# Last block of a small transformer: TensorE's transposes of five operands against VectorE's 32x32 blocks and transfers

## The chip, the core and the metric

The kernel runs on one core of one Trainium2 chip. The metric is the device time of one execution in microseconds, median of several runs.

## The reference

A sequence of 256 tokens with 1024 features goes through two layers (feed-forward, mixer, feed-forward, gated embedding) and then one hybrid block; everything is float32. The change touches the hybrid block alone:

```python
proj = jnp.einsum("bsd,dc->bsc", h, w_in)            # 1024 -> 10240 columns
xc, bg, cg, zc, q, k, v, za, g_conv, g_attn = jnp.split(proj, splits, axis=-1)
c = causal_depthwise_conv(cg * xc, conv_w)            # width 3, along the sequence
y_conv = jnp.einsum("bsc,cd->bsd", jax.nn.silu(zc) * bg * c, w_out_conv)
o = mixture_of_dilations(q, k, v, slopes)             # 16 heads of 64, three dilations
y_attn = jnp.einsum("bsc,cd->bsd", jax.nn.silu(za) * o, w_out_attn)
g_conv = jax.nn.sigmoid(g_conv + b_merge[:D_MODEL])
g_attn = jax.nn.sigmoid(g_attn + b_merge[D_MODEL:])
merged = g_conv * y_conv + g_attn * y_attn
return jnp.einsum("bsd,de->bse", merged, w_o)
```

At 256 tokens the three dilations reduce to one attention in which each key counts `times` times (a table of 0 to 3).

## The kernel before

**Weights.** All weights stream through one ring of slots; a slot is a 512-column, 512-row piece (1 MB) of some matrix. SP (SyncE's queue) loads a slot into `w_raw` (3 places) in two transfers of 512 KB, as soon as the slot three before it has been split. ScalarE rounds it to float32r (`w_hi`, `round_hi`, 6 places), GpSimd subtracts to get the rest (`w_lo`, `subtract`, four instructions per slot), and TensorE forms every product as three matmuls: high by high, low by high, high by low (`across_tile`: 4 k-tiles x 3 = 12 matmuls of 512 columns for a slot and one of the two token tiles of 128). ScalarE works four slots ahead (`ahead`).

**The hybrid block.** `HI` is the input projection: 20 column groups c of 512, two slots each, so slots 0 to 39 with slot = 2c + j; then `HC`, `HA` and `HO`, four slots each. `H_ORDER` sets which columns come as which c: 0 and 1 are queries, 2 and 3 keys, 4 and 5 values, 6 x 7 and 8 x 9 the convolution's input, 10 x 11 and 12 x 13 the convolution's gate, 14 and 15 the attention's gate, 16 to 19 the merging gates. Slots 0 to 3 are used for tile 0 and then for tile 1; from slot 4 on a slot is used for both tiles in turn, and the same for all engines: each engine's function `hybrid` walks through c and j and does what the tables name there. After a slot from c = 5 on comes `step(k)`, k = 0 to 20: for TensorE the scores of heads k and k + 1 (even k below 16) and the product of head k - 5's weights with the values; for ScalarE the exponentials of head k; for VectorE scores plus distance and maxima of head k, sums and transposition of head k - 1, and the scaling of head k - 5's output. Queues are in order, and semaphores tie them together.

**Transposes.** Eight column groups (`H_UNITS`: c = 0, 1, 2, 3, 7, 9, 11, 13) are needed with features on the partitions. `take(c)` on VectorE moves them from the accumulator to `h_s` (two places, `H_PLACE`). Then, at the places in `H_UNITS_AT`, TensorE's `unit(c, t)` turns four 128x128 blocks into the PSUM bank `tb[:, 1]`, once for each tile. From there ScalarE's `units(c)` copies them (queries, keys, convolution input), or VectorE's `z_units(c)` multiplies them onto the convolution (gate). The next group must wait until the bank is free: `pe.wait_ge(h_pl_ready, w)` or `pe.wait_ge(h_z_ready, w - 12)`.

**Heads.** The attention weights of a head are turned in another way already. VectorE turns 32x32 blocks of 128x384 into `h_pb`, which holds a pair of heads (m = h // 2). `turn_heads(m)` on SP, behind the weights of slot 19 + 2m, writes the pair to DRAM (`h_bounce`, four transfers of 96 KB), waits until this has landed, and reads it back into `h_pT` in the transposed order (four transfers, pieces of 32 elements, 128 bytes). Before the first head of the next pair goes into `h_pb`, VectorE waits for the write: `dve.wait_ge(h_bounced, 64 * (h // 2))`.

Of the kernel before, what the change touches and what calls it, by code (L numbers as in the profile page):

```python
# [31 lines left out]
P = 128  # L32
# [58 lines left out]
H_CONVOLVE = {(9, 0): 0, (9, 1): 1, (10, 0): 2, (10, 1): 3, (11, 0): 4, (12, 0): 5, (12, 1): 6, (13, 0): 7}  # L91

H_UNITS_AT = {(2, 0): 0, (2, 1): 1, (3, 0): 2, (4, 0): 3, (8, 1): 7, (10, 1): 9, (12, 1): 11, (14, 1): 13}
# [46 lines left out]
def program(nc, A, out):  # L140
    ctx = ExitStack()
    with ctx:
# [14 lines left out]
        pT_hi = sb("pT_hi", [P, 2, TILES * P], F32R)  # L157
        pT_lo = sb("pT_lo", [P, 2, TILES * P], F32R)
# [3 lines left out]
        causal = sb("causal", [P, LCOLS])  # L162
        upto = sb("upto", [P, P])
        ones = sb("ones", [P, P])
        last_row = sb("last_row", [P, P])
# [16 lines left out]
        def area(at, *shape):  # L182
# [5 lines left out]
            if len(shape) == 3:  # L188
# [55 lines left out]
        h_pb = area(13056, 4, 2 * 3 * 32)  # L244
# [13 lines left out]
        H_UNITS = {0: h_qT[:, 0:4], 1: h_qT[:, 4:8], 2: h_kT[:, 0:4], 3: h_kT[:, 4:8], 7: h_uT[:, 0:4],  # L258
                   9: h_uT[:, 4:8], 11: None, 13: None}
# [76 lines left out]
        def tok(t):  # L336
            return slice(t * P, (t + 1) * P)
# [98 lines left out]
        h_pl_in_psum = sem("h_pl_in_psum")  # L436
        h_pl_ready = sem("h_pl_ready")
# [23 lines left out]
        def _(sp):  # L461
# [76 lines left out]
            def linear(s0, w, cols, halves_first=False, after={}):  # L538
# [5 lines left out]
                for i, (col, j) in enumerate(order):  # L544
# [26 lines left out]
            linear(S["HI"], A["w_in_2"][0], [512 * c for c in H_ORDER],  # L571
                   after={H_TURN_SLOT + 2 * m: m for m in range(AH // 2)})
# [12 lines left out]
        def _(pool):  # L585
# [8 lines left out]
            pool.memset(causal[:], 0.0).then_inc(consts_ready, 1)  # L594
            pool.memset(upto[:], 1.0).then_inc(consts_ready, 1)
            pool.memset(ones[:], 1.0).then_inc(consts_ready, 1)
            pool.memset(last_row[:], 0.0).then_inc(consts_ready, 1)
# [36 lines left out]
        def _(act):  # L634
# [412 lines left out]
            def hybrid():  # L1047
# [17 lines left out]
                def units(c):  # L1065

                    dst = H_UNITS[c]
                    for t in range(TILES):
                        w = H_UNIT_NO[c] + t
                        act.wait_ge(h_pl_in_psum, w + 1)  # L1070
                        nc.scalar.copy(dst[:, :, tok(t)], tb[:, 1, :].rearrange("p (k c) -> p k c", k=4)
                                       ).then_inc(h_pl_ready, 1)
# [1629 lines left out]
```

## Time and profile before

| | |
|---|---|
| median of 3 runs | 1368.77 us (1368.23 to 1369.24) |
| profiled execution, own time | 1369.36 us |
| its span, first to last instruction | 1367.6 us |
| granted TensorE clock over the span | 0.999 |
| TensorE, GpSimd, ScalarE, VectorE busy | 99%, 83%, 48%, 45% of the span |
| 16 DMA engines, SP's queue | 56.0% |

The profiled execution lies 0.6 us above the median, and its span 1.8 us under its own time. A time in a row is counted from the span's start, in us. Matmuls overlap in the records, so that an engine that is busy all the time is not at its peak: what a matmul takes is read from one start to the next. The last block's projection runs from about 1043 to 1291, the last instruction ends at 1367.6.

### The profile page before, as it was taken

What the parts mean: (1) busy time and instruction counts of PE and PEld (TensorE: products, weight loads), DVE (VectorE), ACT (ScalarE), POOL (GpSimd) and SP (SyncE); (2) the same over time, 40 slices, a digit from 0 to 9 for tenths busy, and PEclk for the clock granted to TensorE, in tenths of its full rate; (3) what the DMA queues carried; (4) which work ended last, traced back from release to release, by engine and by line L of the source; (5) the groups of instructions that cost most, each with busy time, mean ns of one, the idle gap of its engine ahead of it and who ended that gap; (6) DMA issues with size and microseconds to landing.
All of it is one profiled execution on the core that took longest, in us unless ns stands there. A gap on an engine that the chain in (4) does not pass through costs nothing.

```text
span 1367.6 us, 19680 instructions
## 1 busy us (share of the span) xinstructions
PE 1351.4 (99%) x6755; PEld 1123.6 (82%) x6755; DVE 615.1 (45%) x1570; ACT 657.4 (48%) x757; POOL 1135.3 (83%) x913
## 2 busy tenths in 40 slices
PE   8999999999999999999999999999999999999997
PEld 6888888888888888888888778888888887778886
DVE  6233344654333356323332885333346235762224
ACT  5444454546444456544444676444446443444531
POOL 5999977849999969899998539999978977779882
PEclk9999999999999999999999999999999999999999
DMA  8666654537666555666555426665546557767540
GB/s 272 216 201 207 206 184 141 187 104 231 196 195 193 185 170 190 198 194 213 185 184 184 139 70 209 209 198 191 184 154 198 188 193 186 225 187 255 187 166 31
DMA packets 190656, 253.27 MB, mean 185 GB/s; under 512 B 34524, under 2 KB 129540, under 8 KB 190468
## 3 DMA queue, kind: packets, MB, share of 16 engines
q1 hardware_dynamic: 188308, 245.72, 56.0%
q10 hardware_dynamic: 2288, 6.75, 1.4%
q8 instruction: 37, 0.61, 0.2%
q14 instruction: 23, 0.19, 0.0%
HBM read 248.24 MB, written 4.19 MB: 185 GB/s over the span
## 4 chain that ended last, share of the span: by engine, by line
POOL 64%; issue 19%; PE 13%; DVE 2%; DMA 1%; ACT 1%; SPq 0%; POOLq 0%; ACTq 0%; DVEq 0%
POOL w_lo L614 64%; PE acc L2006 3%; PE acc L2009 3%; PE acc L2007 3%; DMA w_raw<-in_w_ffn_in 1%; PE tb L2009 1%; PE tb L2006 1%; PE tb L2007 1%; PE gu L2006 1%; PE gu L2007 1%; PE gu L2009 1%; DMA h_bounce<-arena 0%; ACT w_hi L647 0%; SPq L489 0%; PE acc L2063 0%
## 5 line engine op out<-in xcount | busy, mean ns | idle before, releaser
L614 POOL TENSOR_TENSOR w_lo<-w_raw,w_hi 128x512 fp32r<-128x512 f32 x896 | 1130.3, 1312 | 205.3 <-ACT w_hi L647 205.2
L647 ACT CAST w_hi<-w_raw 128x2048 fp32r<-128x2048 f32 x225 | 427.6, 1909 | 143.0 <-DMA w_raw<-in_w_ffn_in 35.1
L2094 PE MATMUL gu<-xT,w_hi 128*128 128x512 f32 x512 | 202.4, 395 | 0.0
L2094 PE MATMUL tb<-xT,w_hi 128*128 128x512 f32 x512 | 202.3, 395 | 0.0
L2006 PE MATMUL acc<-w_hi,xT 128*128 128x512 f32 x496 | 198.4, 400 | 0.0
L2007 PE MATMUL acc<-w_lo,xT 128*128 128x512 f32 x496 | 193.2, 389 | 0.0
L2009 PE MATMUL acc<-w_hi,xT 128*128 128x512 f32 x468 | 182.7, 390 | 0.0
L1333 DVE TENSOR_TENSOR arena<-gu,arena 128x256 f32<-128x256 f32 x64 | 27.2, 424 | 300.4 <-PE gu L2094 300.4
L2100 PE MATMUL tb<-xT,w_lo 128*128 128x256 f32 x512 | 140.3, 280 | 0.0
L2100 PE MATMUL gu<-xT,w_lo 128*128 128x256 f32 x512 | 139.8, 279 | 0.0
L2006 PE MATMUL gu<-w_hi,xT 128*128 128x512 f32 x312 | 123.6, 396 | 1.6 <-ACT xT L679 1.6
L2007 PE MATMUL gu<-w_lo,xT 128*128 128x512 f32 x312 | 121.5, 389 | 0.0
L2100 PEld LDWEIGHTS tb<-xT,w_lo 128*128 128x128 f32 x512 | 96.4, 188 | 20.2
L2100 PEld LDWEIGHTS gu<-xT,w_lo 128*128 128x128 f32 x512 | 96.2, 188 | 19.1
L2006 PEld LDWEIGHTS acc<-w_hi,xT 128*128 128x128 f32 x496 | 93.2, 188 | 19.0 <-issue 1.2
L2007 PEld LDWEIGHTS acc<-w_lo,xT 128*128 128x128 f32 x496 | 93.3, 188 | 18.2 <-issue 0.2
L2041 PE MATMUL acc<-w_hi,hidden_T 128*128 128x512 f32 x336 | 104.4, 392 | 0.0
L2044 PE MATMUL acc<-w_lo,hidden_T 128*128 128x512 f32 x336 | 103.6, 390 | 0.0
L2049 PE MATMUL acc<-w_hi,hidden_T 128*128 128x512 f32 x336 | 103.5, 389 | 0.0
L2009 PEld LDWEIGHTS acc<-w_hi,xT 128*128 128x128 f32 x468 | 87.8, 188 | 19.0
L823 ACT ACTIVATE arena<-gu 128x256 f32<-128x256 f32 x32 | 12.3, 383 | 184.2 <-DVE gu L1336 184.2
L2094 PEld LDWEIGHTS tb<-xT,w_hi 128*128 128x128 f32 x512 | 97.1, 190 | 2.6
(361 smaller groups left out, 1965.4 us busy)
## 6 DMA issues: line engine op xcount, KB each, us to landing
w_raw<-in_w_ffn_in SPq DMA_DIRECT2D x176, 512.0 KB, 4.7
w_raw<-in_w_ffn_out SPq DMA_DIRECT2D x88, 512.0 KB, 4.1
w_raw<-in_w_in SPq DMA_DIRECT2D x80, 512.0 KB, 4.6
w_raw<-in_mlstm_w_in SPq DMA_DIRECT2D x24, 512.0 KB, 4.4
w_raw<-in_w_ple_gate SPq DMA_DIRECT2D x16, 512.0 KB, 4.2
w_raw<-in_w_kv SPq DMA_DIRECT2D x16, 512.0 KB, 4.3
w_raw<-in_mlstm_w_out SPq DMA_DIRECT2D x8, 512.0 KB, 4.4
w_raw<-in_diff_w_q SPq DMA_DIRECT2D x8, 512.0 KB, 4.2
```

Source lines behind the costliest of these rows:

```text
L614: ins = pool.tensor_tensor(w_lo[:, slot.spl, cols], w_raw[:, slot.raw, cols], w_hi[:, slot.spl, cols].bitcast(F32), ALU.subtract)
L647: nc.scalar.copy(w_hi[:, slot.spl, :], w_raw[:, slot.raw, :]).then_inc(hi_ready, 1)
L823: nc.scalar.activation(sg[:, j, :], gate_rows(j)[:, 0:2 * P], ACT.Silu).then_inc(silu_ready, 1)
L1333: v.tensor_tensor(part, low, rs_row, ALU.mult).then_inc(row_step, 1)
L2006: mm(out, xh, wh, start=(half == 0 and k == 0), stop=False)
L2007: mm(out, xh, wl, start=False, stop=False)
L2009: last = mm(out, xl, wh, start=False, stop=(half == 1 and k == 3))
L2041: mm(acc[:, t, 512 * half:512 * half + 512], a_hi[:, k, tok(t)], w(w_hi, half), start=st, stop=False)
L2044: mm(acc[:, t, 512 * half:512 * half + 512], a_hi[:, k, tok(t)], w(w_lo, half), start=False, stop=False)
L2049: last = mm(acc[:, t, 512 * half:512 * half + 512], a_lo[:, k, tok(t)], w(w_hi, half), start=False, stop=sp_)
L2094: return mm(pair_of(j), w_hi[:, slot.spl, at:at + P], xT[:, 4 * half + k, :, :].rearrange("p a c -> p (a c)"), start=(half == 0 and k == 0 ...
L2100: return mm(pair_of(j)[:, 0:2 * P], w_lo[:, slot.spl, at:at + P], xT_hi[:, 4 * half + k, :], start=False, stop=False)
```

## The change

TensorE's `unit`, ScalarE's `units` and VectorE's `z_units` are gone. Right behind `take(c)`, VectorE's `turn_unit(c)` turns 32x32 blocks of the unit (two instructions of 128x512) into a buffer `h_blocks[c]`. SP writes it to DRAM (`store_unit`: four transfers of 128 KB) and later reads it back into its place (`load_unit`: four transfers, pieces of 128 bytes), at the slots in `H_STORE_UNITS` and `H_LOAD_UNITS`. The convolution's gate lands in `h_za` (the place of the embedding's operand) and `h_zb`, and `gate_conv(c)` multiplies it on in one instruction. The block buffer of the heads has a second copy in the place of the constant tables, which the last block does not use: VectorE waits for the write of the pair before the last one. `turn_heads(m)` is split: `store_heads(m)` behind slot 19 + 2m, `load_heads(m)` behind slot 20 + 2m. The convolutions sit at other slots, and `b_merge` is loaded in two halves.

The diff, cut to its core:

```diff
-H_CONVOLVE = {(9, 0): 0, (9, 1): 1, (10, 0): 2, (10, 1): 3, (11, 0): 4, (12, 0): 5, (12, 1): 6, (13, 0): 7}
-H_UNITS_AT = {(2, 0): 0, (2, 1): 1, (3, 0): 2, (4, 0): 3, (8, 1): 7, (10, 1): 9, (12, 1): 11, (14, 1): 13}
+H_CONVOLVE = {(10, 0): 0, (10, 1): 1, (11, 0): 2, (11, 1): 3, (13, 0): 4, (13, 1): 5, (14, 0): 6, (14, 1): 7}
+H_GATE_AT = {(15, 0): 11, (17, 0): 13}
+H_UNITS = (0, 1, 2, 3, 7, 9, 11, 13)
+H_BLOCKS_FREE = {7: 3, 9: 7, 11: 0, 13: 11}
+H_STORE_UNITS = {10: (0, 1), 12: (2,), 14: (3,), 22: (7,), 27: (9,), 31: (11,), 33: (13,)}
+H_LOAD_UNITS = {11: (0, 1), 13: (2,), 15: (3,), 23: (7,), 28: (9,), 32: (11,), 35: (13,)}
...
-        h_pb = area(13056, 4, 2 * 3 * 32)
+        h_pb = [area(13056, 4, 2 * 3 * 32), tables[:].rearrange("p a b -> p (a b)").rearrange("p (j n) -> p j n", j=4)]
...
-            def turn_heads(m):
+            def store_heads(m):
                 sp.wait_ge(h_blocks_turned, 2 * m + 2)
+                for i in range(4):
+                    sp.dma_start(h_bounce[m % 2][i].rearrange("(j b) n -> b j n", j=4),
+                                 h_pb[m % 2][32 * i:32 * i + 32]).then_inc(h_bounced, 16)
+            def load_heads(m):
+                if m >= 2:
+                    sp.wait_ge(h_pv_in_psum, 2 * m - 2)
                 if m:
                     sp.wait_ge(h_pt_landed, 64 * m)
...
                 sp.wait_ge(h_bounced, 64 * (m + 1))
...
+            def store_unit(c):
+                sp.wait_ge(h_unit_turned, H_UNIT_NO[c] + 2)
+                for i in range(4):
+                    sp.dma_start(h_unit_bounce[c][i].rearrange("(j b) n -> b j n", j=4),
+                                 h_blocks[c][32 * i:32 * i + 32]).then_inc(h_unit_stored, 16)
+            def load_unit(c):
+                n = H_UNITS.index(c)
+                sp.wait_ge(h_unit_stored, 128 if n < 2 else 64 * (n + 1))
+                if n:
+                    sp.wait_ge(h_unit_landed, 64 * n)
+                to = h_turned[c].rearrange("p k (t n) -> p (k t) n", t=TILES)
+                for i in range(4):
+                    sp.dma_start(to[:, :, 32 * i:32 * i + 32],
+                                 h_unit_bounce[c][i].rearrange("c (n a) -> c n a", a=32)).then_inc(h_unit_landed, 16)
+            def turns_after(i):
+                m = i - H_TURN_SLOT
+                if m >= 0 and m % 2 == 0 and m // 2 < AH // 2:
+                    store_heads(m // 2)
+                if m >= 1 and m % 2 == 1 and m // 2 < AH // 2:
+                    load_heads(m // 2)
+                for c in H_LOAD_UNITS.get(i, ()):
+                    load_unit(c)
+                for c in H_STORE_UNITS.get(i, ()):
+                    store_unit(c)
...
+                act.wait_ge(h_z_ready, 4)
+                act.wait_ge(h_bm_landed, 16)
+                act.dma_start(h_bm[:, 0:D], A["b_merge_2"][:, D:2 * D].broadcast_to([P, D])).then_inc(h_bm_landed, 16)
...
-                        if h >= 2 and h % 2 == 0:
-                            dve.wait_ge(h_bounced, 64 * (h // 2))
+                        if h >= 4 and h % 2 == 0:
+                            dve.wait_ge(h_bounced, 64 * (h // 2 - 1))
...
+                def turn_unit(c):
+                    if c in H_BLOCKS_FREE:
+                        dve.wait_ge(h_unit_stored, 64 * (H_UNITS.index(H_BLOCKS_FREE[c]) + 1))
+                    for t in range(TILES):
+                        dve.wait_ge(h_evac, H_EVAC[c] - 1 + t)
+                        to = h_blocks[c].rearrange("p j (k t a) -> p t k j a", t=TILES, a=32)[:, t]
+                        v.transpose(to, h_s[:, H_PLACE[c], t, :].rearrange("p (k j b) -> p k j b", j=4, b=32)
+                                    ).then_inc(h_unit_turned, 1)
...
-                            pe.wait_ge(h_pl_ready, 8)
+                            pe.wait_ge(h_unit_landed, 192)
+                        elif h == 8:
+                            pe.wait_ge(h_unit_landed, 256)
...
-                            if (c, j) in H_UNITS_AT:
-                                unit(H_UNITS_AT[c, j], t)
```

How this moves instructions shows at three places. First TensorE at the end of slot 21 (c = 10, j = 1, tile 1), before: L2006, L2007 and L2009 are the three matmuls of a k-tile, L2575 is a group of transposes, L2561 to L2563 are the products of a head's weights with its values.

```order
L2006 MATMUL acc<-w_hi,xT 128x512
L2007 MATMUL acc<-w_lo,xT 128x512
L2009 MATMUL acc<-w_hi,xT 128x512
L2575 MATMUL tb<-ident,arena 128x128 x4
L2561 MATMUL gu<-arena,hidden_T 128x64
L2562 MATMUL gu<-arena,hidden_T 128x64
L2563 MATMUL gu<-arena,hidden_T 128x64
```

The same place now; the three matmuls of a k-tile are L2052, L2053 and L2055, the head's products L2609 to L2611.

```order
L2052 MATMUL acc<-w_hi,xT 128x512
L2053 MATMUL acc<-w_lo,xT 128x512
L2055 MATMUL acc<-w_hi,xT 128x512
L2609 MATMUL gu<-arena,hidden_T 128x64
L2610 MATMUL gu<-arena,hidden_T 128x64
L2611 MATMUL gu<-arena,hidden_T 128x64
```

The group of four transposes is gone and nothing has taken its place; there were 16 such groups.

Second SP's queue from the first write of a pair of heads, before: L489 are weights (two instructions per slot), L529 writes a pair, L535 reads it.

```order
L529 DMA h_bounce<-arena 32x4x192 x4
L535 DMA hidden_T<-h_bounce 128x6x32 x4
L489 DMA w_raw<-in_w_in 128x2x512 x4
```

The same stretch now, slots 19 to 24: L500 are weights, L538 writes a pair, L549 reads it, L556 writes a unit, L567 reads it.

```order
L538 DMA h_bounce<-arena 32x4x192 x4
L500 DMA w_raw<-in_w_in 128x2x512 x2
L549 DMA hidden_T<-h_bounce 128x6x32 x4
L500 DMA w_raw<-in_w_in 128x2x512 x2
L538 DMA h_bounce<-tables 32x4x192 x4
L500 DMA w_raw<-in_w_in 128x2x512 x2
L549 DMA hidden_T<-h_bounce 128x6x32 x4
L556 DMA h_unit<-arena 32x4x256 x4
L500 DMA w_raw<-in_w_in 128x2x512 x2
L538 DMA h_bounce<-arena 32x4x192 x4
L567 DMA arena<-h_unit 128x8x32 x4
```

A pair's read no longer follows its write directly: one slot's weights stand between, ahead of the read in the queue, and units stand at some slots.

Third VectorE at the end of slot 23, where c = 11 is taken, now: L1779 scales a head's output, L1822 to L1824 are a convolution, L1812 takes the unit out of PSUM, L1791 turns it.

```order
L1779 TENSOR_TENSOR arena<-gu,arena 128x2x64
L1822 TENSOR_SCALAR arena<-arena,gcol 128x256
L1823 SCALAR_TENSOR_TENSOR arena<-arena,gcol 128x255
L1824 SCALAR_TENSOR_TENSOR arena<-arena,gcol 128x254
L1812 SCALAR_TENSOR_TENSOR arena<-acc,rstd,arena 128x512 x2
L1791 STREAM_TRANSPOSE arena<-arena 128x4x4x32 x2
L1758 SCALAR_TENSOR_TENSOR arena<-rel,gu 128x384
```

Two transposes stand between the taking of the unit and the next head's scores (L1758).

## Rows read from the trace of the kernel before

**Rows 1.** The page: engines' busy time, and the chain's shares by engine.

```profile
PE 1351.4 (99%) x6755; PEld 1123.6 (82%) x6755; DVE 615.1 (45%) x1570; ACT 657.4 (48%) x757; POOL 1135.3 (83%) x913
POOL 64%; issue 19%; PE 13%; DVE 2%; DMA 1%; ACT 1%; SPq 0%; POOLq 0%; ACTq 0%; DVEq 0%
```

**Rows 2.** Stretches: PE, PEld, DVE, ACT, POOL busy; granted clock, DMA share, GB/s.

```profile
1060.00:1100.00 40.00, 40.00 (x193) 33.16 (x192) 7.36 (x15) 18.16 (x16) 36.31 (x30) 1.00 0.59 191
...
1180.00:1200.00 20.00, 19.44 (x101) 15.94 (x101) 17.11 (x38) 12.63 (x16) 16.89 (x13) 1.00 0.64 187
```

**Rows 3.** Timeline (start, us): split of slots 11 and 12, first use of slot 12.

```profile
1087.67 10.02 POOL L614 TENSOR_TENSOR w_lo<-w_raw,w_hi 128x512 fp32r<-128x512 f32 x8 [1.33 <-ACT w_hi L647]
...
1114.24 0.39 PE L2006 MATMUL acc<-w_hi,xT 128*128 128x512 f32 x1
```

**Rows 4.** Groups by line: count | busy us, mean ns | idle before, releaser.

```profile
L2575 PE MATMUL tb<-ident,arena 128*128 128x128 f32 x64 | 9.6, 272 | 1.4 <-DVE arena L1786 0.9 <-ACT arena L1071 0.6
L1738 DVE STREAM_TRANSPOSE arena<-arena 128x384 f32<-128x384 f32 x16 | 9.0, 564 | 16.7 <-DMA h_bounce<-arena 16.7
```

**Rows 5.** Timeline of TensorE: a group of transposes; slots 32 and 33, without one.

```profile
1231.51 0.39 PE L2009 MATMUL acc<-w_hi,xT 128*128 128x512 f32 x1
1231.74 0.60 PE L2575 MATMUL tb<-ident,arena 128*128 128x128 f32 x4
1232.10 0.47 PE L2006 MATMUL acc<-w_hi,xT 128*128 128x512 f32 x1
1232.41 0.39 PE L2007 MATMUL acc<-w_lo,xT 128*128 128x512 f32 x1
...
1247.67 0.39 PE L2006 MATMUL acc<-w_hi,xT 128*128 128x512 f32 x1
...
1253.11 0.39 PE L2006 MATMUL acc<-w_hi,xT 128*128 128x512 f32 x1
```

**Rows 6.** Timeline of TensorE: slot 25, tile 1, from its first matmul.

```profile
1205.49 0.47 PE L2006 MATMUL acc<-w_hi,xT 128*128 128x512 f32 x1
...
1209.38 0.63 PE L2575 MATMUL tb<-ident,arena 128*128 128x128 f32 x4 [0.89 <-DVE arena L1786]
```

**Rows 7.** DMA from 1120 to 1240: queue's share; issues, KB each, median us to landing.

```profile
DMA packets 39507, 25.31 MB, mean 211 GB/s; under 512 B 26176, under 2 KB 30272, under 8 KB 39498
...
q1 hardware_dynamic: 39498, 25.19, 72.3%
...
w_raw<-in_w_in SPq DMA_DIRECT2D x36, 512.0 KB, 4.8
h_bounce<-arena SPq DMA_DIRECT2D x32, 96.0 KB, 4.7
hidden_T<-h_bounce SPq DMA_DIRECT2D x32, 96.0 KB, 2.8
```

**Rows 8.** Timeline of SP's queue: issuing a pair's four writes and four reads.

```profile
1136.14 2.20 SPq L529 DMA_DIRECT2D h_bounce<-arena  x4
1143.84 2.61 SPq L535 DMA_DIRECT2D hidden_T<-h_bounce  x4
```

**Rows 9.** Timeline: split of slot 7; first scores.

```profile
1065.65 5.06 POOL L614 TENSOR_TENSOR w_lo<-w_raw,w_hi 128x512 fp32r<-128x512 f32 x4
...
1107.81 0.93 PE L2545 MATMUL gu<-arena 64*128 64x128 f32 x8
```

**Rows 10.** Timeline: scores of heads 2 and 3, split of slot 17, pair 0's products.

```profile
1119.77 0.93 PE L2545 MATMUL gu<-arena 64*128 64x128 f32 x8
...
1124.66 5.29 POOL L614 TENSOR_TENSOR w_lo<-w_raw,w_hi 128x512 fp32r<-128x512 f32 x4 [1.92 <-ACT w_hi L647]
...
1138.18 0.33 PE L2561 MATMUL gu<-arena,hidden_T 128*128 128x64 f32 x2
```

**Rows 11.** Timeline: pair 7's reads on SP, its products on TensorE.

```profile
1228.89 2.95 SPq L535 DMA_DIRECT2D hidden_T<-h_bounce  x4
...
1235.37 0.33 PE L2561 MATMUL gu<-arena,hidden_T 128*128 128x64 f32 x2
```

More of the change, by code:

```diff
@@ L161, in program @@
         ident = sb("ident", [P, P])
[L162 to L165, printed above, removed]
+        tables = sb("tables", [P, 6, P])
+        causal = tables[:, 0:3].rearrange("p a b -> p (a b)")
+        upto, ones, last_row = (tables[:, i] for i in (3, 4, 5))
         gcol = sb("gcol", [P, 168])
@@ L435, in program @@
         h_evac = sem("h_evac")
[L436 to L437 removed]
+        h_unit_turned = sem("h_unit_turned")
+        h_unit_stored = sem("h_unit_stored")
+        h_unit_landed = sem("h_unit_landed")
         h_scores = sem("h_scores")
@@ L548, in linear @@
                                  src[:, 4 * j + 2 * k:4 * j + 2 * k + 2, col:col + 512]) for k in range(2)])
-                    if i in after:
-                        turn_heads(after[i])
+                    if after:
+                        after(i)
             def ple(name, w_proj, w_gate):
@@ L570, in _ @@
             ple("P1", A["w_ple_proj"][1], A["w_ple_gate"][1])
-            linear(S["HI"], A["w_in_2"][0], [512 * c for c in H_ORDER],
-                   after={H_TURN_SLOT + 2 * m: m for m in range(AH // 2)})
+            linear(S["HI"], A["w_in_2"][0], [512 * c for c in H_ORDER], after=turns_after)
             linear(S["HC"], A["w_out_conv_2"][0], both)
@@ L593, in _ @@
                                pattern=[[-1, P]], channel_multiplier=1).then_inc(ident_ready, 1)
[L594 to L597, printed above, removed]
+            pool.memset(causal, 0.0).then_inc(consts_ready, 1)
+            pool.memset(upto, 1.0).then_inc(consts_ready, 1)
+            pool.memset(ones, 1.0).then_inc(consts_ready, 1)
+            pool.memset(last_row, 0.0).then_inc(consts_ready, 1)
             pool.wait_ge(consts_ready, 4)
@@ L1063, in step @@
                         ins.then_inc(h_exped, 1)
[L1065 to L1072, printed above, removed]
                 steps = 0
@@ L2272, in cumulate @@
                     pe.wait_ge(m_logf, 1)
-                    mm(tb[:, 1, 16:24], upto[:], m_lf, start=True, stop=True).then_inc(m_cum, 1)
+                    mm(tb[:, 1, 16:24], upto, m_lf, start=True, stop=True).then_inc(m_cum, 1)
                 chunk(2, {0: turn_gates, 3: cumulate})
@@ L2280, in spread @@
                         pe.wait_ge(m_am_ready, t)
-                    mm(tb[:, 0, :], ones[:], m_diag, start=True, stop=True).then_inc(m_spread, 1)
+                    mm(tb[:, 0, :], ones, m_diag, start=True, stop=True).then_inc(m_spread, 1)
                 chunk(3, {0: lambda: spread(0)})
                 pe.wait_ge(m_last_rhs, 1)
-                mm(tb[:, 1, 24:32], last_row[:], m_last, start=True, stop=True).then_inc(m_last_in_psum, 1)
+                mm(tb[:, 1, 24:32], last_row, m_last, start=True, stop=True).then_inc(m_last_in_psum, 1)
                 spread(1)
@@ L2564, in step @@
                            ).then_inc(h_pv_in_psum, 1)
-                def unit(c, t):
-                    pe.wait_ge(h_evac, H_EVAC[c])
-                    w = H_UNIT_NO[c] + t
-                    if 0 < w <= 12:
-                        pe.wait_ge(h_pl_ready, w)
-                    elif w > 12:
-                        pe.wait_ge(h_z_ready, w - 12)
-                    for k in range(4):
-                        ins = nc.tensor.transpose(tb[:, 1, tok(k)], h_s[:, H_PLACE[c], t, tok(k)], ident[:])
-                    ins.then_inc(h_pl_in_psum, 1)
                 by_tile(s0, 4, "HI", acc_outs, (lambda: t_of_x("HI", 1, (0,)), None), lambda: t_of_x("HI", 1, (1,)))
```

63 lines of the change are left out of this document (31 added, 32 removed).

## The prediction

> **What bounds the kernel now.** I read the page first. TensorE is busy 99% of the span [rows 1], and where the change acts it is busy 40.00 of 40.00 us and 19.44 of 20.00 us while VectorE has 7.36 and 17.11, and GpSimd 36.31 and 16.89 [rows 2]. The page's chain of work names GpSimd for 64% [rows 1]; this is not the bound, since the chain follows whoever released last, and GpSimd works as far ahead as its buffers allow. Slots 11 and 12 of the last block's weights are split by 1097.69 (1087.67 + 10.02), and TensorE first uses slot 12 at 1114.24 [rows 3]: 16.5 us of slack. So time leaves the kernel if TensorE's queue gets shorter, and comes back wherever TensorE is made to wait. The clock is 1.00 in both stretches [rows 2], which is the upper level, 2.4 GHz.
>
> **What it removes: TensorE's transposes.** There are 8 units x 2 tiles x 4 = 64, in 16 groups of four [rows 4]. Each takes 272 ns in its record, but the records overlap, so I price a group by starts. Without one, 24 matmuls take 1253.11 - 1247.67 = 5.44 us, 0.227 each. With one, from the matmul before the group to the second behind it there are 1232.41 - 1231.51 = 0.90 us where two matmul steps of 0.227 would stand [rows 5]: a group costs 0.45 us, of which 0.08 is the slow first matmul behind it. 16 x 0.45 = 7.1 us. Bounds: 0.36 (start of the group to the next matmul, 5.8 us in all) and the full records (64 x 0.272 = 17.4 us); starts decide, since TensorE is never idle here.
> The Trainium skill ("TensorE: Matmul & The Clock Gate", part 4) gives about 275 ns per transpose in a kernel. The record agrees (272), and by that figure as a price the gain would be 17.6 us; the starts say 7.1.
>
> **What it removes: two waits of the second tile's group.** The group for tile 1 needs tb free: in two places it waited for ScalarE's copy or VectorE's multiplication, 0.6 and 0.9 us of idle [rows 4]. In full the second cost 1209.38 - 1205.49 = 3.89 us where 12 matmuls and the slow start are 2.80: 1.1 us [rows 6]; the other I scale by its idle time to 0.7. Together 1.8 us. Sum of what goes: **8.9 us**.
>
> **What it adds on VectorE.** 16 transposes of 128x512. The nearest row is the 128x384 one, 564 ns [rows 4]; not below that, and 752 ns if all of it scales with size. I take 0.7: 11 us, against four multiplications out of PSUM that become two longer ones out of SBUF (even, within 2 us). Half of the transposes fall into 1060 to 1100, where VectorE is busy 7.36 of 40 us [rows 2]. The other half, 5.6 us, fall among the heads, where it is busy 17.11 of 20. The second block buffer hides them there: the head transposes waited 16.7 us for writes to DRAM [rows 4], because one buffer had to be emptied first. With two the wait is for the pair before last. VectorE ends with some 10 us more room, so I cost it at nothing. With that cover gone, the scores, which wait for VectorE's maxima, would be late by up to 5.6 us. ScalarE loses 12 copies.
>
> **What it adds on the DMA queue.** Per unit four writes and four reads of 128 KB each. The nearest rows are the heads' 96 KB: 4.7 us to landing for a write (behind weights), 2.8 for a read (queue empty), issues of four 2.20 and 2.61 us [rows 7, 8]. Four unit reads therefore issue in 2.6 to 3.5 us and land 5 to 6 us after the first issue. Between 1120 and 1240 the queue holds 16 engines 72.3% of the time, 87 us, for about 25 MB [rows 7]. Four units fall there, 4.2 MB more: 14 us at the mean price, 28 at twice that for pieces of 128 B. The share would become 84 to 96%: busy, and still under the whole.
> The Trainium skill ("VectorE: DVE Perf Modes", the three transpose paths) speaks against this: a plain DMA that transposes by its strides is said to be 19 times slower than the crossbar's. Here 32 elements stay contiguous, and the row for that very pattern is 2.8 us per 96 KB [rows 7]; the rule, if it held for these reads, would have shown in that row.
>
> **Where SP can now be late.** SP (SyncE's queue) issues in order; behind each wait of a store or load stand the next weights. Three places.
> (1) Units 0 to 2 must land before the first scores, 1107.81 now [rows 9], 3.6 us earlier with eight groups gone: 1104.2. Slot 7 is split by 1070.7 [rows 9]; then slot 10's weights (0.9), eight writes (4.4 at most), 3 to land, read 0 (5.9), read 1 issued (3.7), weights, four writes, weights (4), 2 to land, read 2 (5.9): about 1100.5, so 4 us to spare. Weights shift by up to 7 us against 16.5 of slack.
> (2) Pair 0. Scores at 1119.77; slot 17 is split by 1129.95, 10.2 us later; the products that need the pair start at 1138.18 [rows 10], 8.2 us after that, and no transpose stood between. Now the read goes out after the weights that this split releases: 0.9 to issue them, three of four read issues (2.0), 2.8 to land: 5.7 us. If the reads queue behind the megabyte of weights (the second half is issued 0.4 later and takes 4.8 [rows 7]: 5.2), 5.2 + 2.6 = 7.8. It fits by 0.4 to 2.5 us.
> (3) Pairs behind unit traffic, 2 and 7 above all. Pair 7 was read at 1228.89, its last issue some 2.2 us later, landing about 1233.9; its products started at 1235.37 [rows 11], a margin of 1.5. Ahead of it now stand unit 13's four writes (2.2, and a wait for VectorE's turning of that unit) and slot 34's weights (0.9), while the wait for its own write is gone: within 1 us of on time, either way.
> I take **1.3 us** of new waits in all, between nothing and 4.
>
> **Other edits**, at nothing: half of b_merge loads later, behind slot 41's rounding, and lands some 4 us after VectorE could use it, but what VectorE computes from it is needed by TensorE only when `HC` begins, some 10 us later (my estimate from the count of slots between); the tables share one allocation; the convolutions move a few slots later and still end before their gate.
>
> **Sum.** The profiled execution took 1369.36 us (span 1367.6 and 1.8 around it), 0.6 above the median 1368.77. 1369.36 - 8.9 + 1.3 = 1361.8; at the median, **1361.2**.
>
> **Rivals.**
> A. No new wait shows, or up to 4 us of them (the forecast): 1359.9 to 1363.9. 64%.
> B. Several pairs land late, 4 to 6 us in all, since unit reads stand before them: 1364 to 1366. For it: 72.3% may become 96%. Against it: one late pair gives the next one room. 13%.
> C. The change doesn't do what it says: waits of about 6 to 11.6 us give the whole gain back, for example because the first scores wait too. If a unit's read takes 1.7 times 5.9 us, three of them in a row add 12 us, and less the 4 to spare the scores wait 8: 1367.9. With other sizes of it 1366 to 1371.5. 9%.
> D. Slower. Every pair's read lands behind weights and another read. The wait begins when landing takes more than the 8.2 us of (2), and the sign turns at 8.9 / 8 = 1.1 us per pair, that is from 9.3 us on. At 2.2 us per pair: 1368.8 - 8.9 + 17.6 = 1377.5. My bounds for one pair are 5.7 and 7.8; one unit read in front adds up to 3.5, at two or three pairs and not at eight. 11%.
> E. The transposes are worth their full records and nothing waits: 1368.8 - 17.4 - 1.8 = 1349.6. Against it: the starts. 3%.
>
> **The numbers.** About 0.2% (2.7 us) is what a measurement of this kernel tells from no change: the limits are 1366.0 and 1371.5. Faster is A, B and E, 80%; same is C, 9%; slower is D, 11%. The range of 8 in 10 holds A and B and the near edge of C: 1359.0 to 1367.0, with the low end 1 us under "no wait at all" for the error of 0.45 per group.
>
> **What the changed trace would show.** No group of transposes in TensorE's row between slots 4 and 29; a slot with a unit falls from 6.3 to 5.44 us; no idle before a transpose. VectorE's 128x512 transposes at 0.6 to 0.75 us and no 16.7 us of waiting for h_bounce. TensorE waiting for hidden_T<-h_bounce at pairs 0, 2 or 7, 0 to 2 us each. DMA share 84 to 96% between the first head and the last. Wrong would be: idle time before the first scores (reads dearer than 5.9 us), a wait at most pairs (the queue is full), or weights split later than TensorE wants them.

## The result, and the profile after

The changed kernel takes 1375.38 us (median of 6 runs, 1373.38 to 1376.40), the kernel before 1369.01 (6 runs, 1368.23 to 1371.17): ratio 1.004, 95% interval 1.003 to 1.005. It is slower by 6.4 us where 1361.2, faster, was forecast. The profiled execution took 1376.38 us with a span of 1374.6 and a granted clock of 0.994 (1369.36, 1367.6 and 0.999 before).

The page's engines and chain, which answer to [rows 1]:

```profile
PE 1349.3 (98%) x6691; PEld 1120.7 (82%) x6691; DVE 628.3 (46%) x1584; ACT 651.8 (47%) x745; POOL 1138.9 (83%) x913
POOL 66%; issue 20%; PE 9%; DMA 2%; DVE 1%; SPq 1%; ACT 0%; POOLq 0%; ACTq 0%; DVEq 0%
```

Two stretches, as in [rows 2] (PE, PEld, DVE, ACT, POOL busy; clock; DMA share; GB/s):

```profile
1060.00:1100.00 40.00, 40.00 (x179) 33.10 (x178) 13.80 (x29) 12.61 (x7) 32.99 (x27) 1.00 0.81 230
1180.00:1200.00 20.00, 20.00 (x101) 16.35 (x100) 16.30 (x39) 12.55 (x14) 16.01 (x13) 1.00 0.93 240
```

TensorE is busy 2.1 us less, with 6691 matmuls for 6755 (64 transposes gone), and the span grew by 7.0 us all the same: TensorE stands idle some 9 us more. The DMA engines are far busier: 0.81 and 0.93 of these stretches for 0.59 and 0.64.

The groups that answer to [rows 4], and the waits of 1055 to 1280 (us in total, times, longest):

```profile
L1791 DVE STREAM_TRANSPOSE arena<-arena 128x512 f32<-128x512 f32 x16 | 10.4, 685 | 0.0
L1774 DVE STREAM_TRANSPOSE arena<-arena 128x384 f32<-128x384 f32 x8 | 4.5, 558 | 0.0
L1774 DVE STREAM_TRANSPOSE tables<-arena 128x384 f32<-128x384 f32 x8 | 4.5, 558 | 0.0
```

```profile
ACT w_hi L690 <- DMA w_raw<-in_w_in: 67.8, 18, 10.8
...
PE gu L2609 <- DMA hidden_T<-h_bounce: 9.4, 3, 4.7
```

VectorE's 16.7 us of waiting for h_bounce are gone, as forecast. TensorE now waits 9.4 us for pairs of heads, and ScalarE waits 67.8 us for weights where it waited 22.1.

**Where it went, slot by slot.** I take each slot of the last projection from its first matmul (a row of the timeline) to the next slot's first.

| slots | before, us | after, us | |
|---|---|---|---|
| 4, 5, 6 | 6.26, 6.37, 6.37 | 5.44 each | transposes gone |
| 10 | 6.39 | 6.98 | scores wait for a unit |
| 15, 16 | 6.16, 7.53 | 11.28, 8.73 | pair 0 late; low clock behind it |
| 17, 21, 25 | 7.05, 7.81, 8.14 | 6.15 each | transposes and their waits gone |
| 27 | 6.16 | 6.83 | pair 6 late |
| 29, 30 | 7.07, 6.14 | 11.78, 7.59 | pair 7 late; low clock |
| 4 to 35 | 203.53 | 209.01 | +5.5 |
| 36 to the end | 98.19 | 98.20 | |

Against their undisturbed lengths (6.39, 6.16, 7.21, 6.16, 6.16, 6.14) the six late slots cost 0.6 + 5.1 + 1.5 + 0.7 + 5.6 + 1.5 = 15.0 us. With no wait at all slots 4 to 35 would take 194.0. So **9.5 us went, 15.0 came**. The two spans differ by 7.0 us and not by 5.5 because slot 4 starts 1.45 us later in the trace of after (1067.35 for 1065.90); it starts between 1065.9 and 1067.4 in all the kernels profiled here, so I take that part for scatter ahead of the change. Each kernel has one trace: a slot's length is that of one execution.

**Ahead of pair 0.** SP's queue from the first unit write, and TensorE's first scores (start, us; in brackets the idle time before, and who ended it):

```profile
1073.94 5.05 SPq L556 DMA_DIRECT2D h_unit<-arena  x8
...
1081.30 10.88 SPq L567 DMA_DIRECT2D arena<-h_unit  x8
...
1099.84 3.72 SPq L567 DMA_DIRECT2D arena<-h_unit  x4
...
1106.11 0.93 PE L2593 MATMUL gu<-arena 64*128 64x128 f32 x8 [0.53 <-DMA arena<-h_unit]
```

The scores start when unit 2 has landed, at about 1106.1. The forecast had it land at 1100.5, which is 1101.9 with the 1.45 us of scatter. SP is some 4 us behind the schedule of the prediction before pair 0 begins.

**Pair 0.** SP's queue, ScalarE's and GpSimd's split, and TensorE, on the timeline of after:

```profile
1104.83 2.28 SPq L556 DMA_DIRECT2D h_unit<-arena  x4
1107.15 1.42 SPq L500 DMA_DIRECT2D w_raw<-in_w_in  x2
1111.19 4.42 SPq L567 DMA_DIRECT2D arena<-h_unit  x4
1115.66 7.53 SPq L500 DMA_DIRECT2D w_raw<-in_w_in  x6
...
1121.34 1.92 ACT L690 CAST w_hi<-w_raw 128x2048 fp32r<-128x2048 f32 x1 [3.51 <-DMA w_raw<-in_w_in]
...
1123.33 5.31 POOL L657 TENSOR_TENSOR w_lo<-w_raw,w_hi 128x512 fp32r<-128x512 f32 x4 [1.04 <-ACT w_hi L690]
...
1127.34 6.32 POOL L657 TENSOR_TENSOR w_lo<-w_raw,w_hi 128x512 fp32r<-128x512 f32 x5
...
1133.69 0.90 SPq L500 DMA_DIRECT2D w_raw<-in_w_in  x2
1135.01 3.83 SPq L549 DMA_DIRECT2D hidden_T<-h_bounce  x4
...
1136.25 0.39 PE L2055 MATMUL acc<-w_hi,xT 128*128 128x512 f32 x1
1140.87 0.69 PE L2609 MATMUL gu<-arena,hidden_T 128*128 128x64 f32 x2 [4.24 <-DMA hidden_T<-h_bounce]
...
1142.17 0.77 PE L2052 MATMUL acc<-w_hi,xT 128*128 128x512 f32 x1
...
1143.17 0.63 PE L2055 MATMUL acc<-w_hi,xT 128*128 128x512 f32 x1
1143.60 0.63 PE L2052 MATMUL acc<-w_hi,xT 128*128 128x512 f32 x1
```

SP first stands until 1111.18 (unit 3's write must land), then takes 4.42 us to issue that unit's reads, and only at 1115.66 the weights of slot 16. ScalarE waits 3.51 us for them. The row at 1127.34 ends with slot 17's split, at 1133.66. The same heads' scores began at 1118.07, so the split comes 15.6 us behind them, where it was 10.2 before [rows 10]. It releases slot 20's weights, then pair 0's reads. Their landing is what TensorE waits for: it stands from 1136.6 to 1140.87, 4.24 us.

**The clock behind it** (columns as above):

```profile
1135.00:1142.00 7.00, 2.76 (x14) 2.15 (x12) 3.52 (x9) 3.54 (x4) 7.00 (x7) 0.76 1.00 246
1142.00:1144.00 2.00, 2.00 (x6) 1.64 (x7) 1.55 (x4) 0.00 (x0) 2.00 (x3) 0.50 1.00 361
...
1146.00:1148.00 2.00, 2.00 (x11) 1.65 (x10) 0.00 (x0) 0.00 (x0) 2.00 (x3) 1.00 0.95 328
```

After the wait TensorE is busy without a gap, yet its matmuls start 0.43 us apart (1143.17 to 1143.60) instead of 0.227: the granted clock is 0.50, its lower level (1.2 GHz). That is the 1.5 us of slot 16, and some 0.6 us more in the pair's products (1140.87 to 1142.17 is 1.30; 0.70 in experiment 5, at the upper level). Pair 7 and slot 30 show the same: about 4 of the 15.0 us are the clock.

**Pair 7**, SP's queue:

```profile
1220.93 2.90 SPq L567 DMA_DIRECT2D p_T<-h_unit  x4
...
1225.20 2.28 SPq L538 DMA_DIRECT2D h_bounce<-tables  x4
1230.69 1.76 SPq L556 DMA_DIRECT2D h_unit<-arena  x4
1232.49 0.98 SPq L500 DMA_DIRECT2D w_raw<-in_w_in  x2
1233.59 4.59 SPq L549 DMA_DIRECT2D hidden_T<-h_bounce  x4
```

And a wait of SP's, 1100 to 1245:

```profile
SPq L556 <- DVE arena L1791: 3.2, 1, 3.2
```

SP stands 3.2 us until VectorE has turned unit 13, ahead of slot 34's weights and of pair 7's reads, which start 4.7 us later than before [rows 11] while TensorE needs them at the same time (it falls idle at 1235.4; its products started at 1235.37 before).

### The profile page after: what moved, and what is told of

Read it like the earlier page. It is cut to its first block, busy times and chain, and to the rows that moved or that the text cites. A ratio compares the mean times of both kernels' runs of the same rounds, so it can differ in the third digit from the quotient of the medians.

```text
span 1374.6 us, 19610 instructions
## 1 busy us (share of the span) xinstructions
PE 1349.3 (98%) x6691; PEld 1120.7 (82%) x6691; DVE 628.3 (46%) x1584; ACT 651.8 (47%) x745; POOL 1138.9 (83%) x913
## 4 chain that ended last, share of the span: by engine, by line
POOL 66%; issue 20%; PE 9%; DMA 2%; DVE 1%; SPq 1%; ACT 0%; POOLq 0%; ACTq 0%; DVEq 0%
POOL w_lo L657 66%; PE acc L2052 2%; PE acc L2055 2%; PE acc L2053 2%; DMA w_raw<-in_w_ffn_in 1%; DMA hidden_T<-h_bounce 1%; PE tb L2055 1%; PE tb L2053 1%; PE gu L2053 1%; PE tb L2052 1%; PE gu L2055 1%; PE gu L2052 1%; SPq L500 0%; SPq L549 0%; PE acc L2109 0%
## 5 line engine op out<-in xcount | busy, mean ns | idle before, releaser
L2052 PE MATMUL acc<-w_hi,xT 128*128 128x512 f32 x496 | 198.7, 401 | 0.0
L2053 PE MATMUL acc<-w_lo,xT 128*128 128x512 f32 x496 | 194.2, 392 | 0.0
L2055 PE MATMUL acc<-w_hi,xT 128*128 128x512 f32 x468 | 183.5, 392 | 0.0
L2052 PE MATMUL gu<-w_hi,xT 128*128 128x512 f32 x312 | 123.6, 396 | 2.2 <-ACT xT L722 2.2
L2053 PE MATMUL gu<-w_lo,xT 128*128 128x512 f32 x312 | 121.5, 389 | 0.0
L2052 PEld LDWEIGHTS acc<-w_hi,xT 128*128 128x128 f32 x496 | 94.0, 190 | 19.9 <-issue 1.2
L2053 PEld LDWEIGHTS acc<-w_lo,xT 128*128 128x128 f32 x496 | 94.1, 190 | 18.8 <-issue 0.2
L2055 PEld LDWEIGHTS acc<-w_hi,xT 128*128 128x128 f32 x468 | 88.5, 189 | 19.1
```

Of the source, the lines that this page charges most:

```text
L2052: mm(out, xh, wh, start=(half == 0 and k == 0), stop=False)
L2053: mm(out, xh, wl, start=False, stop=False)
L2055: last = mm(out, xl, wh, start=False, stop=(half == 1 and k == 3))
```

## The experiments

Times are medians; "4 to 35" is the sum of those slots in the profiled run. My theory: SP, by its order and the short pieces of the unit reads, brings single pairs late. Rivals: the head half of the change does it; or the queue is simply full.

**1. The heads' half alone.** The kernel before, TensorE's transposes kept; `turn_heads` is split as in the change.

```diff
-        h_pb = area(13056, 4, 2 * 3 * 32)
+        h_pb = [area(13056, 4, 2 * 3 * 32), tables[:].rearrange("p a b -> p (a b)").rearrange("p (j n) -> p j n", j=4)]
...
-                   after={H_TURN_SLOT + 2 * m: m for m in range(AH // 2)})
+                   after=turns_after)
```

> One part alone: the heads' second block buffer and the read one slot behind the write; TensorE keeps its transposes of the units. Theory (the reads of pairs 0 and 7 come late because unit traffic holds SP's queue and delays the weights they stand behind): without unit traffic no pair is waited for by more than 0.5 us, the 16.7 us of VectorE's waits for h_bounce go, and since TensorE hardly waited before, the time is 1367 to 1369.5. Rival (the read behind a slot's weights is itself the cost): 3 to 5 us of waits for hidden_T, 1372 to 1374.

1370.71 us, ratio 1.0006 (0.9997 to 1.0015); 4 to 35: 203.62 against 203.53. VectorE's wait for h_bounce is gone, and TensorE waits 0.6 us for pairs. The time lies above its range, but the kernel before ran at 1369.80 beside it: worth nothing, harmless. The loss needs the units.

**2. The units' half alone.** After, with one block buffer, so that a pair is written and read together.

```diff
-                        if h >= 4 and h % 2 == 0:
-                            dve.wait_ge(h_bounced, 64 * (h // 2 - 1))
-                        to = h_pb[(h // 2) % 2][:, :,
+                        if h >= 2 and h % 2 == 0:
+                            dve.wait_ge(h_bounced, 64 * (h // 2))
+                        to = h_pb[0][:, :,
...
-                if m >= 1 and m % 2 == 1 and m // 2 < AH // 2:
+                if m >= 0 and m % 2 == 0 and m // 2 < AH // 2:
                     load_heads(m // 2)
```

> The other part alone: units by VectorE's blocks and transfers, heads as before (one block buffer, write and read together behind slot 19 + 2m). Theory: early unit traffic still delays the splits, but a pair's read does not stand behind weights, so pair 0 is late by less than 2 us and pair 7 by up to 5; 1363 to 1369. Rival (the DMA queue is simply full, share over 90%): waits of 10 us and more as in the changed kernel, 1373 to 1378.

1383.33 us, ratio 1.0108 (1.0086 to 1.0129); 4 to 35: 217.78. Slower than expectation and rival alike. Waits of 1055 to 1280:

```profile
ACT w_hi L690 <- DMA w_raw<-in_w_in: 80.3, 21, 10.1
DVE arena L1774 <- DMA h_bounce<-arena: 45.0, 7, 12.1
PE gu L2609 <- DMA hidden_T<-h_bounce: 6.5, 2, 3.6
```

VectorE's wait for the one buffer grew from 16.7 to 45.0 us. So the second buffer does what it should, and is needed as soon as the units are on the queue. How much of the 14 us is the buffer was not isolated: here SP also stands 35.6 us (1110 to 1250) until pairs' writes have landed, with the next weights behind it, and experiments 6 and 7 show that this costs time by itself.

**3. Unit 13 written behind pair 7's read.**

```diff
-H_STORE_UNITS = {10: (0, 1), 12: (2,), 14: (3,), 22: (7,), 27: (9,), 31: (11,), 33: (13,)}
+H_STORE_UNITS = {10: (0, 1), 12: (2,), 14: (3,), 22: (7,), 27: (9,), 31: (11,), 34: (13,)}
```

> The changed kernel with unit 13's write one slot later, behind pair 7's read instead of before slot 34's weights. Theory: pair 7's wait (5.6 us, and 1.4 us of lower clock behind it) goes, pair 0's stays: 1367.5 to 1370. Rival (full queue): the same bytes, the same time, 1374 to 1376.

1369.45 us, ratio 0.9994 (0.9983 to 1.0005); 4 to 35: 202.90. Slot 29 fell from 11.78 to 7.24 and slot 30 from 7.59 to 6.14; pair 0 stayed (11.51 and 8.75). SP's queue:

```profile
1226.52 1.04 SPq L500 DMA_DIRECT2D w_raw<-in_w_in  x2
1230.49 2.60 SPq L549 DMA_DIRECT2D hidden_T<-h_bounce  x4
1233.14 2.08 SPq L556 DMA_DIRECT2D h_unit<-arena  x4
```

The reads go out 3.1 us earlier (2.2 counted from where TensorE needs them, since this trace runs ahead by the rest) and take 2.6 us to issue instead of 4.6. The edit takes the wait for VectorE and unit 13's four writes out of the way together; it does not tell them apart.

**4. The early units pulled apart**, so that less stands ahead of slot 17's weights.

```diff
-H_STORE_UNITS = {10: (0, 1), 12: (2,), 14: (3,), 22: (7,), 27: (9,), 31: (11,), 33: (13,)}
-H_LOAD_UNITS = {11: (0, 1), 13: (2,), 15: (3,), 23: (7,), 28: (9,), 32: (11,), 35: (13,)}
+H_STORE_UNITS = {10: (0, 1), 12: (2,), 16: (3,), 22: (7,), 27: (9,), 31: (11,), 33: (13,)}
+H_LOAD_UNITS = {11: (0,), 12: (1,), 13: (2,), 17: (3,), 23: (7,), 28: (9,), 32: (11,), 35: (13,)}
```

> The changed kernel with units 1's read one slot later and unit 3's write and read two slots later, so that SP meets finished transfers. Theory: slots 12 to 17 are split earlier, pair 0's wait (5.1 us, and 1.5 us of lower clock) falls to under 1.5 us, pair 7's stays: 1368.5 to 1371. Rival (full queue): 1374 to 1376. Second rival (pair 0 is late since its read stands behind weights, whenever these are split): a wait of 3 us or more stays.

1370.84 us, ratio 1.0012 (1.0003 to 1.0020); 4 to 35: 205.27. Slot 15 fell to 7.89, slot 10 to 6.39, and pair 7 stayed (11.81 and 7.87). The time is as expected; pair 0's wait fell to 1.7 us, not under 1.5, and slot 16 (8.81) kept all of its lower clock.

**5. Both tables together**: the edits of 3 and 4.

> The changed kernel with both moves of the two runs before: unit 13's write behind pair 7's read, unit 1's read one slot later, unit 3's write and read two slots later. Theory (the waits come from what stands in SP's queue, each for itself): pair 0's wait as in the run with the early units apart (1.7 us, and 1.6 of lower clock), pair 7's as in the run with the last unit later (1.1): slots 4 to 35 in 199 us where the kernel before needs 203.5, time 1364.5 to 1366. Rival (full DMA queue): what is freed at one place is lost at the next, 1369 or more.

1367.79 us, ratio 0.9986 (0.9977 to 0.9994); 4 to 35: 199.83. The two repairs add: 3.74 + 6.11 = 9.85 forecast by the single runs, 9.18 measured. The time missed its range by some 2 us. What is left is slot 15 (7.37), slot 29 (7.76), slot 27 (6.64) and a new one, slot 19 (8.63, pair 2).

**6 to 8. A pair's read issued ahead of its slot's weights**: on 5, on the changed kernel, and on 5 with unit 3 written behind slot 18 and read behind slot 21.

```diff
+                if first:
+                    first()
                 for view, src in halves:
...
-                if m >= 1 and m % 2 == 1 and m // 2 < AH // 2:
-                    load_heads(m // 2)
```

> The run before plus: a pair's read is issued ahead of its slot's weights, behind the same wait for the split. Theory (the read stands behind a megabyte of weights): it lands 1 to 3 us earlier, no pair is waited for by more than 0.3 us, slots 4 to 35 in 194.5 to 196 us, time 1360 to 1362. Rival (the weights ahead of the read do not matter, since the engines share out what is queued): the same as the run before, 1364.5 to 1366.

> The changed kernel with the pair's read ahead of its slot's weights and nothing else. Theory (two causes add up: the read stands behind weights, and SP comes late to it since it is held at unit traffic): pair 0's wait falls from 5.1 to 2 to 3.5 us, pair 7's from 5.6 to 3 to 4.5; 1370 to 1373. Rival (order alone is the cause): no wait left, 1360 to 1362. Second rival (order does not matter): 1374 to 1376.

> As the run with both tables and the read first, but unit 3 is written behind slot 18 and read behind slot 21 (heads 8 and on need it), so that nothing of the units stands in SP's queue between slots 14 and 17. Theory: slots 16 and 17 are split as early as in the kernel before relative to the scores, pair 0 is in time; slots 4 to 35 in 194.1 to 195 us, time 1359.5 to 1361.5. Rival: with the reads first nothing was left to win, and unit 3 now delays pair 1: 1361 to 1364.

1374.23, 1379.25 and 1375.66 us; ratios 1.0033 (1.0020 to 1.0046), 1.0068 (1.0055 to 1.0081), 1.0045 (1.0027 to 1.0063); 4 to 35: 204.40, 212.65, 207.97. All three missed. In 6 pair 0 is in time (slot 15: 6.16), but pair 2 stays late (slot 19: 8.52) and slots 25 and 26 take 9.73 and 8.69. SP's longest wait there, 1110 to 1245:

```profile
SPq L549 <- DMA h_bounce<-tables: 19.9, 4, 6.4
```

With the other buffer's 7.9 us SP stands 27.8 us for the pairs' own writes, against 11.9 in experiment 5. That wait now stands ahead of the weights, which go out late (ScalarE waits 79.0 us for them, 60.3 in 5). The weights between write and read are what fills that wait.

**9. The unit transfers on ScalarE's queue**, at slots 4 to 30 of its own walk (both tables change with it, and the functions move to ScalarE).

```diff
-                    sp.dma_start(h_unit_bounce[c][i].rearrange("(j b) n -> b j n", j=4),
+                    act.dma_start(h_unit_bounce[c][i].rearrange("(j b) n -> b j n", j=4),
```

> The changed kernel with all unit writes and reads issued by ScalarE on its own queue, at slots 4 to 30, so that SP carries weights and heads alone. The same bytes in the same pieces cross the same 16 engines. Theory (what costs is SP: it issues in order, waits for landings and for VectorE there, and a full queue holds it; the weights and pairs behind come late): no wait over 0.5 us for a pair but pair 0 or 7 once, slots 4 to 35 in 194.5 to 198 us, time 1360.5 to 1364.5 beside 1370 before. Rival (the engines are full): waits of 5 us and more stay, 1369 to 1376, and the share stays over 90%.

1374.93 us, from 1367.46 to 1382.14 over 12 runs, ratio 1.0035 (1.0018 to 1.0051); 4 to 35: 208.71. Pair 7 is in time (slot 29: 6.16), pair 0 is not (10.72), and slot 25 takes 10.99. Missed; the waits say why:

```profile
ACT w_hi L668 <- issue: 38.8, 10, 11.2
...
ACT w_hi L668 <- DMA arena<-h_unit: 7.6, 1, 7.6
```

ScalarE rounds the weights; issuing and waiting for transfers now holds it, and so the splits (in the changed kernel it has no idle time put down to issue there). The holding changed engines.

**10. Units read in long pieces**: 1 KB instead of 128 B, same bytes. This leaves out the second half of the units' transposition.

```diff
-                    sp.dma_start(to[:, :, 32 * i:32 * i + 32],
-                                 h_unit_bounce[c][i].rearrange("c (n a) -> c n a", a=32)).then_inc(h_unit_landed, 16)
+                    sp.dma_start(h_turned[c][:, i, :], h_unit_bounce[c][i]).then_inc(h_unit_landed, 16)
```

> The changed kernel with the units read back in 1 KB pieces into contiguous places instead of 128-byte ones; this leaves out the second half of the transposition, so that the output is not the reference's. Same bytes, same waits, same places in SP's queue, 128 x 8 x 4 x 8 = 32768 small pieces become 4096. Theory (SP is held at round trips and by the number of descriptors still queued): a unit's read no longer holds SP (3.2 us of gap inside unit 13's four read issues goes), pair 0's wait falls from 5.1 to 2 to 4 us, pair 7's from 5.6 to 3 to 5; 1369 to 1373. Rival (only waits on semaphores hold SP): pairs as late as before, 1374 to 1376. Second rival (small pieces are the whole cost): 1360 to 1363.

1369.66 us, ratio 0.9999 (0.9990 to 1.0008); 4 to 35: 202.09. Slot 15 took 6.56, slot 16 7.21: of pair 0's 6.6 us 6.2 went with the short pieces (4.7 in experiment 12, where slot 15 took 8.11 with the same queue up to there). The time is in its range, but the expectation was wrong on pair 7, which was to gain too and stayed (11.31 and 7.72): SP still stands 4.1 us there for VectorE. A unit read's median from issue to landing, 1060 to 1130, first after, then this kernel:

```profile
arena<-h_unit SPq DMA_DIRECT2D x16, 128.0 KB, 3.8
```

```profile
arena<-h_unit SPq DMA_DIRECT2D x16, 128.0 KB, 2.9
```

The Trainium skill ("VectorE: DVE Perf Modes", the three transpose paths) puts a plain DMA that transposes by strides at 19 times the crossbar's cost when the innermost stride of its destination is large. Short pieces cost 1.3 times the long ones per transfer here, so I read these two rows as no case of that rule; no run here used the crossbar's path.

**11. Experiment 5 with unit 7 read behind pair 2** and not ahead of it.

```diff
-H_LOAD_UNITS = {11: (0,), 12: (1,), 13: (2,), 17: (3,), 23: (7,), 28: (9,), 32: (11,), 35: (13,)}
+H_LOAD_UNITS = {11: (0,), 12: (1,), 13: (2,), 17: (3,), 24: (7,), 28: (9,), 32: (11,), 35: (13,)}
```

> The better of the tables so far, with one entry moved: unit 7 is read behind slot 24 (behind pair 2's read) instead of behind slot 23 (ahead of it). In the run with both table edits pair 2 was read at 1159.03, behind unit 7's read (1152.51 to 1156.69), and slot 19 took 8.63 us where an undisturbed one takes 6.15. Theory (what stands ahead of a pair's read on SyncE's queue decides whether it is late): slot 19 falls to 6.15 to 6.9, slots 4 to 35 take 197.4 to 199 us instead of 199.83, and the time is 0.8 to 2.5 us below that run's 1367.8, ratio to before 0.9965 to 0.998. Slot 15 (7.37) and slot 29 (7.76) stay, within 0.7. Rival (the queue is simply full, so any order costs the same): slot 19 falls, and another slot between 20 and 29 grows by as much; slots 4 to 35 stay at 199.5 to 200.5.

**1364.73 us**, ratio **0.9965** (0.9951 to 0.9979); 4 to 35: 196.29. This beats both kernels. Slot 19 fell from 8.63 to 6.15. SP's queue in 5, then in 11:

```profile
1152.51 4.85 SPq L567 DMA_DIRECT2D arena<-h_unit  x4
1157.40 1.17 SPq L500 DMA_DIRECT2D w_raw<-in_w_in  x2
1159.03 4.54 SPq L549 DMA_DIRECT2D hidden_T<-h_bounce  x4
```

```profile
1152.34 0.90 SPq L500 DMA_DIRECT2D w_raw<-in_w_in  x2
1155.19 3.70 SPq L549 DMA_DIRECT2D hidden_T<-h_bounce  x4
1159.33 3.22 SPq L567 DMA_DIRECT2D arena<-h_unit  x4
```

The pair's reads start 3.8 us earlier, the unit's 6.8 later, and nobody waits for the unit. The gain is larger than expected (slots 4 to 35 in 197.4 to 199). Not all of the 3.5 us between the two runs is this edit: slot 15 (6.35 for 7.37) has the same queue ahead of it in both and differs by run, more than the 0.7 allowed for; slot 29 gave 0.5. Slot 21 grew by 0.6, far less than the full-queue rival asks. The queue itself, 1120 to 1240 in experiment 11:

```profile
q1 hardware_dynamic: 59681, 29.91, 94.6%
```

This is the fullest queue of all kernels here, in the fastest that computes the whole function; it is 90.7% in the changed kernel and 78.3% in experiment 2, the slowest. A full queue by itself is not what costs.

**12. Experiments 10 and 3 together** (leaves out the same half of the transposition).

> Leaves out the second half of the units' transposition, as the run with long pieces did: the units are read in pieces of 1 KB. In addition unit 13 is written behind slot 34, and so behind pair 7's read. Two causes are to account for all that came back: the short pieces of the unit reads with what they delay (slot 15 fell from 11.28 to 6.56 when they went), and the wait for VectorE's turning of unit 13 ahead of pair 7 (slot 29 fell from 11.78 to 7.24 when it moved). Theory (the two are separate and add): slots 4 to 35 take 202.09 less 3.5 to 5.2 for slot 29 and 1.6 for slot 30: 195.3 to 197.0 us, against 194.1 with no wait at all; the time is 1362 to 1364.5, ratio 0.9945 to 0.997. This is what I had predicted for the change itself within 3 us. Rival (a full queue, whatever its pieces): a wait shows at other pairs instead, and slots 4 to 35 take 199 us or more.

1362.61 us, ratio 0.9947 (0.9933 to 0.9960); 4 to 35: 196.78, within the 195.3 to 197.0 expected. TensorE's waits for pairs, 1055 to 1280:

```profile
PE gu L2607 <- DMA hidden_T<-h_bounce: 2.0, 2, 1.7
```

The two edits take away 12.2 of the 15.0 us. The time is within 1.4 us of the forecast 1361.2, but this kernel leaves out half of the turning: it shows what the two causes cost, not that the change can reach it.

## Why the prediction was wrong

**What goes: right.** 8.9 us forecast, 9.5 measured; slots 4, 5, 6 and 8 fell by 0.82 to 0.93 us for two groups each, to 5.44, so pricing a group by starts (0.45) held, and the full records (17.4 us) are refuted. The 275 ns per transpose of the Trainium skill ("TensorE: Matmul & The Clock Gate", part 4), stated there for a kernel in bf16, agree with the record; as a price they would have given 17.6 us, and the trace shows 9.5 with the waits.

**VectorE: right for TensorE.** 0.7 us for the new transpose, 0.685 measured; its wait fell from 16.7 us to nothing. Experiment 1 shows the waits it lost had cost nothing, and experiment 2 that the cover is real. What was not priced is SP, which waits for VectorE too: see step (3).

**The queue's share: right, and misleading.** 84 to 96% forecast; the DMA view of 1120 to 1240 answers to [rows 7]:

```profile
q1 hardware_dynamic: 54408, 29.09, 90.7%
...
w_raw<-in_w_in SPq DMA_DIRECT2D x36, 512.0 KB, 4.8
hidden_T<-h_bounce SPq DMA_DIRECT2D x32, 96.0 KB, 4.1
```

A pair's read lands in 4.1 us, not 2.8. Issuing four took 3.83 us at pair 0 and 4.59 at pair 7. The forecast took 2.61 for it, the row of pair 1; pair 0's own row in the trace of before already shows 4.00, and pair 7's 2.95 [rows 11]:

```profile
1129.37 4.00 SPq L535 DMA_DIRECT2D hidden_T<-h_bounce  x4
```

Still, from the end of slot 17's split to the products it took 7.2 us (1133.66 to 1140.87), inside the 5.7 to 7.8 of step (2): one pair's price held.

**Step (1), first scores: 4 us short, and saved by its margin.** "About 1100.5, so 4 us to spare": the unit landed at 1106.1, and the scores waited 0.5 us. No single term is far off. Units 0 and 1 took SP 10.88 us from first to last read issue where the sum had 9.6, the eight writes 5.05 for 4.4, and the stretch from there to unit 2's reads 7.7 for 6. That the wait was small is luck: the margin happened to be as large as the error. SP goes on to pair 0 with this delay. "Weights shift by up to 7 us against 16.5 of slack" weighed the shift against TensorE's use alone. That slack did hold; TensorE never waited for weights.

**Step (2), pair 0: the step that failed.** "Slot 17 is split by 1129.95, 10.2 us later" was carried over from the trace of before. The shift of weights that step (1) had just allowed moves this very split, and the split releases SP for the pair's reads. With 10.2 now 15.6, 5.4 us are added to a margin of 0.4 to 2.5, which gives 3 to 5 us late; 4.24 us of idle came. The text had the shift (up to 7 us) and the margin; the sum was not made. Experiments 4 and 10 show it from both sides: with fewer or cheaper unit transfers ahead of slot 17's weights, pair 0's wait falls.

**Step (3), pair 7: failed too.** "Within 1 us of on time" named "a wait for VectorE's turning of that unit" and gave it no price. It held SP 3.2 us, and the read itself took 2.0 us longer to issue than in experiment 3. There, with the wait and the writes behind the read, 6.0 of pair 7's 7.1 us go. Pair 2, named beside it, was in time in the changed kernel (slot 19: 6.15) and late in experiments 5 and 6.

**The sum** had 1.3 us of new waits, "between nothing and 4"; 15.0 came. About 4 of them are the lower clock, a term the prediction did not have. Rival B had the mechanism (single pairs late behind unit reads) at 4 to 6 us. Rival D, the slower one, had the sign but not the place: 2 pairs late by about 5 us, not 8 by 2.2.

**What stays open**: why pair 0 misses by 0.2 to 2 us in runs whose queue is the same up to there (slot 15: 7.37 and 6.35 in experiments 5 and 11, 6.56 and 8.11 in 10 and 12). Half of b_merge's later load showed no cost: VectorE waits 5.6 us for it, and slots 36 to the end take 98.20 for 98.19.

## What to carry to other kernels

When transfers are added to a queue that issues in order, redo the schedule of everything that the queue releases: slack against the consumer of the weights says nothing about the slack of what is issued behind them. Put each read that a busy engine will wait for ahead of work that can wait, and no wait for another engine in front of it; but leave between a write and its read the transfers that fill the wait for landing (experiments 6 to 8, without them, took 4 to 8 us more than the kernels they started from). Here five entries of two tables (the changed kernel against experiment 11), with the same instructions, are worth about 10 us (ratios 1.004 and 0.9965 to the kernel before), as much as everything that the change removed; and moving the traffic to ScalarE's queue did not pay, since ScalarE had weights to round.

## What the runs showed of the hardware

- Issuing can hold the engine that issues: within four reads of a unit SP needed 0.6 and 0.7 us for the first two and 2.5 for the third (row at 1111.19, 4.42 us for four), and 3.81 us for two of pair 6's reads at 1217.02. In experiment 9 three of a unit's reads held ScalarE 5.49 us (at 1191.57). That it is pieces still queued which hold it is my inference; for it speaks that the same four reads took 1.78 us in long pieces (experiment 10, at 1106.33).
- Idle time of TensorE costs more than its length: behind 4.24 us of it the clock was at 0.50 for more than 3 us of work, and some 2 us were lost. It isn't decided by the length alone in these runs: behind 1.45 us (experiment 4) it fell to 0.50 too, behind 2.21 (experiment 5) and 1.68 (experiment 12) it stayed at 1.00.
- VectorE's transposes by 32x32 blocks took 558 ns at 128x384 and 684 (median) at 128x512, with GpSimd busy 83% of the span.
